# Seven products for eight in the FFN's up projections, seven forms of its input, and one placement of TensorE's buffers modulo 512 bytes

## What is computed

```python
def swiglu_ffn(h, w_gu, w_down):
    gate, up = jnp.split(h @ w_gu, 2, axis=-1)
    return (jax.nn.silu(gate) * up) @ w_down

for layer in range(DEPTH):
    h = rms_norm(x, mix_norm[layer])
    ...
    x = x + y
    x = x + swiglu_ffn(rms_norm(x, ffn_norm[layer]), ffn_w_gu[layer], ffn_w_down[layer])
return rms_norm(x, final_norm)
```

## Time and profile before

| | us |
|---|---|
| median of three runs | 2890.85 (2888.9 to 2892.37) |
| span of the profiled execution | 2891.1 |
| TensorE busy | 2838.0 |
| VectorE busy | 1110.7 |
| GpSimd busy | 1018.6 |
| ScalarE busy | 549.3 |

### The profile page before, as it was taken

How to read it: one execution, slowest core, us unless ns; L and a number is a source line. 1 busy time by engine, 2 the same in 40 slices (tenths; PEclk the granted TensorE clock), 3 DMA queues, 4 the chain that set the end, 5 groups by cost and what they waited for, 6 DMA issues and landing times.

```text
span 2891.1 us, 35190 instructions
## 1 busy us (share of the span) xinstructions
PE 2838.0 (98%) x12673; PEld 2340.1 (81%) x12673; DVE 1110.7 (38%) x1594; ACT 549.3 (19%) x920; POOL 1018.6 (35%) x1423
## 2 busy tenths in 40 slices
PE   7999999999999999999999999999989999999998
PEld 6888888888887888888888788787878888888887
DVE  7423323323324322333322536447462332233234
ACT  3220220220224010100001423414441001010002
POOL 3323323323323333333333345254323333333332
PEclk9999999999999999999999999999999999999999
DMA  3102102102101111111111111111111111111112
GB/s 129 41 29 66 41 30 66 41 30 66 41 29 38 48 49 50 47 47 47 47 47 50 41 45 53 35 54 41 37 34 48 48 47 47 48 50 47 47 47 91
DMA packets 173478, 140.02 MB, mean 48 GB/s; under 512 B 8656, under 2 KB 142928, under 8 KB 173392
## 3 DMA queue, kind: packets, MB, share of 16 engines
q1 hardware_dynamic: 171664, 133.53, 15.4%
q10 hardware_dynamic: 1728, 5.26, 0.5%
HBM read 133.51 MB, written 5.24 MB: 48 GB/s over the span
## 4 chain that ended last, share of the span: by engine, by line
PE 94%; DVE 3%; ACT 2%; issue 1%; DMA 0%; SPq 0%; DVEq 0%; ACTq 0%
PE ps L429 31%; PE ps L433 31%; PE ps L432 31%; PE ps L488 1%; DVE residual L998 1%; DVE uc L1213 0%; DVE xn L954 0%; DVE residual L1289 0%; PE ps L556 0%; ACT gate_buf L679 0%; ACT L866 0%; ACT L860 0%; DMA residual<-in_x 0%; DVE gate_buf L1218 0%; DVE uc L1208 0%
## 5 line engine op out<-in xcount | busy, mean ns | idle before, releaser
L429 PE MATMUL ps<-h_hi,w_hi 128*128 128x512 f32 x2048 | 801.1, 391 | 5.3 <-DVE uc L1197 3.2
L433 PE MATMUL ps<-h_hi,w_lo 128*128 128x512 f32 x2048 | 797.8, 390 | 0.0
L432 PE MATMUL ps<-h_lo,w_hi 128*128 128x512 f32 x2048 | 797.7, 389 | 0.0
L350 POOL TENSOR_TENSOR small<-w_raw 128x1 f32<-128x1 f32 x464 | 104.1, 224 | 1782.9 <-PE ps L429 1767.6
L361 POOL TENSOR_TENSOR w_lo<-w_raw,w_hi 128x512 fp32r<-128x512 f32 x460 | 605.2, 1316 | 36.8
L998 DVE TENSOR_TENSOR residual<-ps,residual 128x512 f32<-128x512 f32 x480 | 329.1, 690 | 347.7 <-PE ps L433 345.2
L429 PEld LDWEIGHTS ps<-h_hi,w_hi 128*128 128x128 f32 x2048 | 385.2, 188 | 86.5 <-issue 3.2
L433 PEld LDWEIGHTS ps<-h_hi,w_lo 128*128 128x128 f32 x2048 | 384.9, 188 | 80.8
L432 PEld LDWEIGHTS ps<-h_lo,w_hi 128*128 128x128 f32 x2048 | 385.2, 188 | 79.3
L429 PE MATMUL ps<-w_hi,a_hi 128*128 128x512 f32 x816 | 322.2, 395 | 0.8 <-DVE uc L1197 0.8
L432 PE MATMUL ps<-w_lo,a_hi 128*128 128x512 f32 x816 | 322.0, 395 | 0.0
(11 more groups left out here) (185 smaller groups left out, 2827.6 us busy)
## 6 DMA issues: line engine op xcount, KB each, us to landing
w_raw<-in_ffn_w_gu SPq DMA_DIRECT2D x176, 256.0 KB, 2.9
w_raw<-in_ret_w_in SPq DMA_DIRECT2D x96, 256.0 KB, 2.8
w_raw<-in_ffn_w_down SPq DMA_DIRECT2D x88, 256.0 KB, 2.6
w_raw<-in_lru_w_in SPq DMA_DIRECT2D x48, 256.0 KB, 2.9
w_raw<-in_ret_w_out SPq DMA_DIRECT2D x32, 256.0 KB, 2.6
w_raw<-in_lru_w_out SPq DMA_DIRECT2D x24, 256.0 KB, 2.7
residual<-in_x SPq DMA_DIRECT2D x8, 512.0 KB, 6.8
out_y<-residual SPq DMA_DIRECT2D x8, 512.0 KB, 2.6
```

The source lines that it names most:

```text
L350: nc.gpsimd.tensor_tensor(small[:, 62:63], col, col, ALU.subtract)
L429: m = nc.tensor.matmul(o, l_hi, r_hi, start=start, stop=False)
L432: nc.tensor.matmul(o, l_hi, r_lo, start=False, stop=False)
L433: return nc.tensor.matmul(o, l_lo, r_hi, start=False, stop=stop)
```

## The change

*Products.* The gate and up tiles of one pair, and the two halves of the width, form a 2 x 2 matrix of weight units (`p11` gate first half, `p21` up first half, `p22` up second half, `p12` gate second half); the two halves of the width and of the tokens form a 2 x 2 matrix of the input. Seven products of 12 matmuls (four blocks along half the width, times three) take the place of 96 matmuls. Products 4, 5 and 6 are added onto the banks of products 0, 1 and 2:

```diff
+            def product(n, u, p):
+                j, form = PRODUCTS * u + p, H_OF[p]
+                w_h, w_l = f_unit(j)
+                pe.wait_ge(f_wready, n * F_UNITS + j + 1)
+                for k in range(4):
+                    w, r = slice(k * P, (k + 1) * P), h_cut(form, k)
+                    m = three(f_bank(u, p), w_h[:, w], w_l[:, w], H_hi[:, r], H_lo[:, r],
+                              p < 4 and k == 0, k == 3, onto=p >= 4)
+                m.then_inc(f_mm, 1)
...
+                if p == 4:
+                    pe.wait_ge(f_t, 2 * n + u + 1)
+                elif p == 5:
+                    pe.wait_ge(f_ev, n * F_EV + 7 * u + E_T5 + 1)
+                elif p == 6:
+                    pe.wait_ge(f_ev, n * F_EV + 7 * u + E_T7 + 1)
```

*Weights.* A chunk has 18 units (7 for each pair, 4 for down) in a ring of three of its own. SP loads into eight slots. GpSimd makes four sums or differences for each pair and all rest parts; ACT makes the rounded parts (it was GpSimd), each when the product three units earlier is done:

```diff
+                f_add(one, p21, p22, ALU.add)
+                f_lo_of(units, j, p11)
+                pool.wait_ge(f_summed, sums + 1)
+                f_add(p21, p11, p21, ALU.subtract)
+                f_lo_of(units, j + 1, one)
+                pool.wait_ge(f_wready, units + j + 1)
+                f_add(two, one, p11, ALU.subtract)
+                f_lo_of(units, j + 2, p21)
...
+                f_add(one, two, p12, ALU.subtract)
+                f_lo_of(units, j + 3, two)
+                pool.wait_ge(f_summed, sums + 4)
+                f_lo_of(units, j + 4, p12)
+                if meanwhile is not None:
+                    meanwhile()
+                f_lo_of(units, j + 5, p22)
+                f_lo_of(units, j + 6, one)
```

```diff
+                    dve.wait_ge(f_t, 2 * n + u + 1)
+                    for e, p in ((E_T5, 1), (E_T7, 2), (E_T6, 3)):
+                        dve.wait_ge(f_mm, mms + p + 1)
+                        if e:
+                            dve.wait_ge(f_ev, evs + e)
+                        TT(t, f_bank(u, p), t, ALU.add).then_inc(f_ev, 1)
...
+                    TT(c21, t, f_bank(u, 1), ALU.subtract).then_inc(f_ev, 1)
...
+                    TT(s1, s1, c21, ALU.mult).then_inc(f_act, 1)
...
+                    TT(c12, t, f_bank(u, 2), ALU.subtract).then_inc(f_ev, 1)
+                    lower(n, u, 0)
...
+                    TT(s2, c12, s2, ALU.mult).then_inc(f_ev, 1)
...
+                    TT(s2, s2, t, ALU.mult).then_inc(f_act, 1)
+                    lower(n, u, 1)
```

```diff
+        sb("fill_small", 104)
...
+        dk = sb("decay_sb", 520)
+        sb("fill_decay", 120)
```

More of the change, by code:

```diff
@@ L308, in into @@
                     src = rows(lru_w_in[0], kh, (0 if gate else LRU) + g * (GT * P) + tile * P)
-                    load(j % RING, src, None if waited and j == 0 else last(u0 + j, j, False))
+                    load(j % RING, src, None if waited and j == 0 else last(u0 + j, j, restart))
             def outof(g, u0):
@@ L382, in ffn @@
                 with pool.Fori(1, CHUNKS - layer) as c:
-                    chunk(c, False)
+                    chunk(c)
                 if layer == 1:
-                    u0, before = UB_FFN[1] + (CHUNKS - 1) * CHUNK_UNITS, [(CHUNKS - 1) * 4 + n for n in landed]
-                    units(8, u0, before)
-                    for j in range(8, CHUNK_UNITS):
-                        split(j % RING, 16 * (before[j % RING] + j // RING + 1), u0 + j, None, last_out(j - 8))
-            ffn(0, landed)
@@ L392, in _ @@
[L392 to L393 removed]
+                    chunk(CHUNKS - 1, last=True)
+            ffn(0)
+            pool.wait_ge(f_mm, chunk_no(0, CHUNKS - 1) * F_MM + 2 * PRODUCTS)
             nc.gpsimd.memset(wri_raw[:], 0.0).then_inc(wri_zero, 1)
@@ L813, in _, with lam_exp, ffn_norm_of @@
+            def lam_exp():
+                act.wait_ge(lam_e, 1)
+                nc.scalar.activation(small[:, 12:24], small[:, 0:12], ACT.Exp).then_inc(lam_sp, 1)
+            def ffn_norm_of(layer):
+                for j in range(3):
+                    w_round(chunk_no(layer, 0), j)
+                stats(2 * layer + 1)
+                act.wait_ge(n_rstd, 2 * layer + 3)
+                forms(layer)
+            ffn_norm_of(0)
             ffn(0)
@@ L1122, in chunk @@
                         for s in range(SB):
-                            add(base + 8 + nh * 8 + s, 8 + nh * 8 + s, s, nh)
-                with dve.Fori(0, CHUNKS - layer) as c:
+                            dve.wait_ge(f_mm, n * F_MM + 2 * PRODUCTS + nh * 9 + s + 2)
+                            f_add(s, nh, s)
+                chunk(0, between=(lambda: None) if layer else lam_min)
+                if layer == 0:
+                    lam_log()
+                with dve.Fori(1, CHUNKS - layer) as c:
                     chunk(c)
@@ L1151, in _ @@
+            forms(0)
             ffn(0)
```

575 lines of the change are left out of this document (438 added, 137 removed).

## The result

The changed kernel takes **2812.06 us** (median of 4 runs, 2810.54 to 2815.13) against 2889.88 before: ratio 0.9732, 95% interval 0.972 to 0.9743. Forecast were 2827, range 2810 to 2858: the direction and the range hold, the middle is 15 us too slow. The profiled execution's span is 2813.3 us, where the sum of the prediction says 2827.5.

The account below looks back on a forecast made before the run. TensorE bounds the kernel: a number of matmuls times their pace, plus the places where it stands. 2891.1 - 119.8 - 19 + 61 + 4.4 + 10.5 - 0.7 = 2827.5 us of span, forecast 2827 us, range 2810 to 2858.

Parts of the forecast that it names:

- What bounds the kernel: Whole kernel: TensorE, busy 2838.0 of 2891.1 us; time is matmuls times their pace, plus the places where TensorE stands.
- parts 1 and 2: FFN chunks: 528 matmuls fewer, -119.8 us; mixed-operand groups: 3300 matmuls speed up once all buffers are aligned alike, -19 us.
- Part 3: Two FFN norms: TensorE waits for the first products' forms, product 2 starting late; 30.5 us more each, +61 us together.
- the walk: FFN norm: step-by-step timing from the first scaled block; products 0, 1, 2 start at +9.4, +19.6, +42.1 us.
- Part 4: Steady FFN chunk: GpSimd, slowed by DVE, delivers rest part 10 slightly late; 0.2 us a chunk, 22 times, +4.4 us.
- The slower rival: FFN chunk: the port shared with DVE makes GpSimd the bound, 4.4 us a chunk, 97 us, so 2920 us; chance 5%.
- Part 5: Last chunk: TensorE stands 7.5 us for all four down weights, then loses about 3 at half clock; +10.5 us.
- Part 6: LRU norm: GpSimd's memset and first weights come before the scaling rather than beside it; -0.7 us.
- slower rivals: FFN chunk: GpSimd becomes the bound, 2920 us, 5%; or a milder stall of 0.9 us a chunk, 2843 us, 12%.
- the missing alignment gain: Mixed-operand matmuls: aligning the buffers brings nothing, so the time is 2846 us; chance 7%.
- Norms hide: FFN norms: making the forms stays hidden, so a norm still costs 11.8 us and the time is 2766 us; chance 3%.

Follow-up runs that it names:

- last_early: Changed kernel with ACT rounding the last chunk's last two down weights earlier, right behind the third activation's rounding; TensorE still waits for all four: 2810.49 us.
- last_units: Changed kernel with the last chunk's last two down weights rounded earlier and TensorE awaiting each down weight where first needed, first products reordered: 2802.93 us.

## Why the prediction was right, and where it was off

**What bounds the kernel, and parts 1 and 2**: right to a few tenths. The time is a number of matmuls times their pace, the removed ones leave by 0.2267 each, and the reading of two paces from the allocation is confirmed by the run with alignment alone (19.35 us, -19 forecast). The period was read too wide, 512 instead of 256 bytes, and one row was misread: 857.46:901.63 holds 190 of the 192 output matmuls, so their pace was 0.2325 there and not 0.2301 (the whole stretches take 44.7 to 44.9 us). The sum had used 0.2325 for all mixed pairs, so the term did not suffer.

**Part 3, the norms**: mechanism right, size 8.7 us too high. Product 2 started at +40.4 instead of +42.1, ahead of it products 0 and 1 at +8.3 and +18.0 for 9.4 and 19.6: the walk came out 1.7 us too long. It was 2.2 too long up to weight 4's rest part (done at +30.9 for +33.1), half of that already ahead of product 0, and 0.6 too short in the seven pieces, of which two last 1.7 us and not 1.27. With the 0.4 us ahead of the walk, which did not come, this is half of the error. The other half is the base: I took 48 matmuls for the stretch to 924.33. The earlier trace rows says x105; 64 of these are transposes and one is the last matmul of the stage before, so there are 40, worth 9.1 us. The norm cost 13.6 to 13.9 us before, not 11.8, and the change therefore added 26.3 and 26.0, not 30.5. That GpSimd's order is the cause is shown by the two runs that change an order alone.

**Part 4, the chunk**: the step that failed is that GpSimd stands in full (5 x 0.68 us) for DVE's instructions with two SBUF operands. In a chunk of the changed kernel rest part 10 starts at 1259.56 and three of the eight pieces up to it take 1.73 to 1.75 us instead of 1.29, so GpSimd lost 3 x 0.45 = 1.35 us, not 3.4. The count was wrong as well as the size: of DVE's five instructions three come in between, the fourth ends only behind part 10, and the fifth begins behind it. GpSimd's rows:

```profile
1253.66 1.73 POOL L466 TENSOR_TENSOR f_w_lo<-f_sum,f_w_hi 128x512 fp32r<-128x512 f32 x1
...
1256.60 1.30 POOL L466 TENSOR_TENSOR f_w_lo<-f_raw,f_w_hi 128x512 fp32r<-128x512 f32 x1
1257.85 1.75 POOL L469 TENSOR_TENSOR f_sum<-f_sum,f_raw 128x512 f32<-128x512 f32 x1
1259.56 1.74 POOL L466 TENSOR_TENSOR f_w_lo<-f_sum,f_w_hi 128x512 fp32r<-128x512 f32 x1
```

DVE's instructions get longer by more, 1.78 us for 0.68, as these rows of it show:

```profile
1256.67 1.78 DVE L1538 TENSOR_TENSOR f_act_lo<-gate_buf,f_act_hi 128x512 fp32r<-128x512 f32 x1 [0.58 <-ACT f_act_hi L1061]
1258.37 1.78 DVE L1530 TENSOR_TENSOR gate_buf<-gate_buf 128x512 f32<-128x512 f32 x1
1260.18 1.67 DVE L1532 TENSOR_TENSOR gate_buf<-gate_buf 128x512 f32<-128x512 f32 x1
```

The rows read as turns. Each of DVE's three ends 0.55 us after the GpSimd instruction that was running when it began (1258.45 after 1257.90, 1260.15 after 1259.60, 1261.85 after 1261.30), and where GpSimd follows at once, its next one is longer by 0.45. Its first long one, at 1253.66, began 0.17 us behind an instruction of DVE's that took 0.75. In the whole trace of the changed kernel DVE has 236 FFN instructions that read two SBUF tiles; 90 of them last over 0.9 us, and each of the 90 ends 0.55 us after the GpSimd instruction beside it.

Part 10 was ready 14.3 us after product 3 (15.9 to 16.7 forecast) with 16.3 to go. The Trainium skill (SBUF — State Buffer, Who interferes with whom) says that such instructions exclude each other for their whole length. The trace agrees, with the turns above. The error was in the count and in the price of a turn, 0.45 us to GpSimd and not 0.68. The slower rival did not come: GpSimd was never the bound in a chunk, and it took three more pieces (5.3 us) to lose the gain, 50 us of it by standing and most of the rest by the clock behind it.

**Part 5, the last chunk**: right, 10.4 for 10.5 us, with both halves near their forecast (7.1 us of standing for 7.5, 3.3 lost behind it for 3).

**Part 6, the LRU norm**: direction right, size -3.0 for -0.7. The step that was mis-sized is what GpSimd's place costs DVE: I counted only the memset's time, while its copies and rest parts beside DVE's scaling had nearly doubled that, 3.95 for 2.07 us. The run with the weights held back gives 1.9 of the 3.0 us for this (0.7 ahead of the stretch, 1.2 in it), with the memset where it was. Most of the other 1.1 us is a shorter time at half clock, and that is chance: at this norm the changed kernel's instructions have 3.4 us of it in `last_early` and 6.8 in `last_units`, which differ in the last chunk alone. The order was not quite as forecast either: the memset and one weight come before the scaling, at 1581 to 1584 us, the next two behind it, from 1604.12 on.

Neither of the slower rivals came, nor the missing alignment gain. "Norms hide" is refuted by 20.4 us of waits.

## What to carry to other kernels

Before a gain or loss is taken from a stretch, count its instructions by kind: an "x105" with 64 transposes in it, taken for 48 products where there were 40, was worth 1.8 us of error twice. Where one engine waits on pieces of another, look first at the order in that queue: moving two lines gave 8 us a norm, while raising TensorE's clock as it waited gave half a microsecond. And a stall of TensorE is to be priced with what follows it: 2.6 us of waiting cost 4.5 in most chunks.

## What the runs showed of the hardware that I had not expected

- For a 512-column matmul the operands' distance modulo 256 bytes sets the pace: 0.2267 us at 0 and at 256, 0.2289 at 64, 0.2333 (up products), 0.2325 (down products of the kernel before) or 0.2329 to 0.2337 (its retention's output) at 128.
- A GpSimd and a DVE instruction that both read two SBUF tiles take turns: DVE's, begun beside one of GpSimd's, ended 0.55 us after it in all 90 cases in which it lasted over 0.9 us (1.78 us for 0.68), and GpSimd's next was longer by 0.45 (1.74 for 1.29). A scaling on DVE with one SBUF tile as input is also slowed by GpSimd work beside it (five in 3.95 for 2.07 us).
- After a stall of 2.6 us the granted clock fell in 14 chunks out of 19 and stayed in 5; with 36 filler matmuls in a norm's gaps it stayed at 1.00 from the first filler on, where it had fallen to 0.54 without them.
